# Dilated mixer: scores and outputs by residues modulo 4 in quarters of the array, with resident bias tables

## The chip, the cores and the metric

The kernel runs on one core of one Trainium2 chip. The metric is the device time of one execution in microseconds; the kernel before has a median of 881.81 us over three runs (881.51 to 882.02).

## What is computed

A batch of one sequence with 256 tokens of 1024 features passes two hybrid layers (retention, sparse attention and a gated recurrence side by side) and then a second block of two layers, all in float32. The first mixer of the second block is the dilated one, and it is where this change is:

```python
DSW_GROUPS = ((128, 1), (512, 4), (2048, 16))       # window, dilation
qkv = (h @ w_qkv).reshape(B, S, 3, G, Hg, HEAD_DIM) # 3 groups of 8 heads of 64
q, k = rmsnorm(q, q_gain), rmsnorm(k, k_gain)
# per group g: query t attends to t - dilation*i, i = 0..window/dilation
logits = q.k * SCALE + bias[t5_bucket(distance), 8*g + head]   # masked outside of the band
o_g, lse_g = softmax_attend(logits, v)
wts = softmax(stack(lse_g))                          # over the three groups
o = sum_g wts_g * o_g;  h = h + o @ w_o
```

A softmax over groups of softmaxes is one softmax over the logits of all three groups, and that is how both kernels compute it, head by head. With 256 tokens group 0 sees the last 129 tokens, group 1 every fourth token back to the start, and group 2 every sixteenth. So a query of groups 1 and 2 only meets keys that have its own residue modulo 4.

## The kernel before

Every engine has its own program, written out by hand; semaphores tie them. TensorE does the dense products as three fp32r products each (high by high, high by low, low by high part; lines 810 to 812 and 841 to 843). Weights come in chunks of 128x2048 through SyncE's queue; ScalarE writes the high part of a chunk (`split_hi`, L1465), VectorE the low part (`split_lo`, L1967), into a ring of four.

The dilated mixer starts with six blocks of 512 columns for q and k ("dsw" blocks 0 to 5; VectorE normalizes each, `qk_norm`), and the three v blocks 6 to 8. While the v blocks run, TensorE folds q and k to features by tokens (`fold`, 12 times 4 transposes, L758), copied out by ScalarE (L1683) and VectorE (L2334). Heads go in pairs p = 0 to 3 (e is the head of the pair, and its 64 features are one half of the rows of the array).

- `dil_pair_scores(p)`: per head, each of the three groups takes 256 keys for the second 128 queries (L1086) and 128 keys for the first 128 (L1093). Products of the masked pairs are computed too.
- `logits(u)` on VectorE: per head one operation on 768 and one on 384 columns (L2344) adds the bias and takes the row maximum. The bias tables have room for four heads; GpSimd brings each head's table from DRAM (`bias_vec`) once the head four before is done (L749).
- `softmax(u)` on ScalarE: exponentials of 768 and 384 columns (L1690, L1691). `scaled(u)` on VectorE divides by the sums (L2354 to L2356).
- `dil_transposes(u, g)`: three 128x128 transposes per head and group, copied out by ScalarE (L1696) or VectorE (L2360).
- `dil_output(p, g)`: the weighted sums of v (L1124, L1126), the two heads in two halves of the array's columns. `dil_high` and `dil_low` (L1675, L2326) then make the high and low parts for the product with `w_o` (block "dswo", `tokens(o, ...)`).

The order of all this on each engine is written in three functions called `dilated`, and each engine waits in that order. TensorE may begin `dil_transposes(0, 0)` only when ScalarE has emptied bank 0 of the last v block, `take(f + 8, 0)` (L1488), and `dil_transposes(1, 0)` after `take(f + 8, 1)`.

Early, in the first input block, VectorE adds bias rows and masks (`bias_vectors`, L2141, L2142), GpSimd writes them to `bias_vec` (L687, L688), and both ScalarE and VectorE wait for those transfers (`vec_out`) ahead of the sparse attention of layer 0 (before L1771 and L2470).

```python
for g in range(3):
    for e in range(2):
        o = dil_scores(e)[0][:, S * g:S * g + S]
        mm = pe.matmul(o.rearrange("p (t n) -> p t n", t=2), q(e, g, 1), k(e, g, slice(0, 2)), start=True, stop=True)
```

## Time and profile before

| what | value |
|---|---|
| median of three runs | 881.81 us |
| the profiled execution | 881.71 us |
| its span | 879.9 us |
| TensorE busy | 872.1 us (99%), 5546 products |
| VectorE, ScalarE busy | 620.2 us (70%), 491.7 us (56%) |
| GpSimd busy | 40.4 us (5%) |
| chain that ended last | TensorE 86%, VectorE 4%, ScalarE 4%, DMA 2% |

The execution's own time holds 1.8 us around its span. A product of float32 operands (not fp32r) stands in the trace as two instructions, so six calls of `pe.matmul` in a loop are a row with x12. Starts of consecutive rows of TensorE give what a piece costs there; the durations overlap.

### The profile page before, as it was taken

The numbers are of one execution on the slowest core, as the hardware profiler recorded it, in microseconds if no ns is written. First come the engines' busy times: TensorE is split into PE (matmuls) and PEld (weight loads), VectorE is DVE, ScalarE is ACT, GpSimd is POOL, SyncE is SP. The second block draws the span as 40 slices with busy tenths as digits, with TensorE's granted clock in tenths as the row PEclk, the third lists the DMA queues.
The fourth block names the chain that finished last, engine by engine and source line by source line (L and its number), as shares of the span: only waits on it lengthen the run. The fifth ranks groups of instructions, "written<-read, shape, count | busy, mean of one in ns | idle before, by whom it ended". The sixth has DMA issues, their size and how long they took to land.

```text
span 879.9 us, 13709 instructions
## 1 busy us (share of the span) xinstructions
PE 872.1 (99%) x5546; PEld 750.2 (85%) x5546; DVE 620.2 (70%) x1064; ACT 491.7 (56%) x742; POOL 40.4 (5%) x69
## 2 busy tenths in 40 slices
PE   9999999999999999999999999999999999999998
PEld 7887888987888888878999988888777899998886
DVE  5889987989988987776666644466778586664441
ACT  6566836667847654576555533355667565553330
POOL 1700010000000000100000000010000000000000
PEclk9999999999999999999999999999999999999999
DMA  8963255742344678623555565565553286555540
GB/s 299 332 230 112 99 192 149 240 144 97 104 160 168 239 233 228 185 74 126 191 183 187 186 202 196 196 191 189 168 168 120 96 279 195 189 182 194 170 156 24
DMA packets 79454, 155.54 MB, mean 177 GB/s; under 512 B 5644, under 2 KB 7852, under 8 KB 79392
## 3 DMA queue, kind: packets, MB, share of 16 engines
q1 hardware_dynamic: 75200, 142.81, 48.9%
q0 software_dynamic: 4192, 11.86, 5.1%
q8 instruction: 44, 0.72, 0.3%
q14 instruction: 18, 0.15, 0.0%
HBM read 153.55 MB, written 1.11 MB: 176 GB/s over the span
## 4 chain that ended last, share of the span: by engine, by line
PE 86%; DVE 4%; ACT 4%; issue 2%; DMA 2%; POOL 1%; SPq 0%; DVEq 0%; ACTq 0%
PE ps L810 17%; PE ps L812 16%; PE ps L811 16%; PE ps L841 9%; PE ps L842 8%; PE ps L843 8%; PE ps_mid L758 2%; DVE w_lo L1967 2%; ACT w_hi L1465 2%; DMA w_raw<-in_w_in 1%; PE ps_mid L1004 1%; PE ps L758 1%; PE ps_mid L1034 1%; PE ps_mid L810 1%; ACT y_tok L1600 1%
## 5 line engine op out<-in xcount | busy, mean ns | idle before, releaser
L1967 DVE TENSOR_TENSOR w_lo<-w_raw,w_hi 128x2048 fp32r<-128x2048 f32 x133 | 299.7, 2260 | 144.0 <-ACT w_hi L1465 143.8
L1465 ACT ACTIVATE w_hi<-w_raw 128x2048 fp32r<-128x2048 f32 x133 | 250.8, 1891 | 189.9 <-PE ps L812 141.5
L810 PE MATMUL ps<-w_hi,act_hi 128*128 128x512 f32 (+1 forms) x446 | 177.6, 398 | 0.8 <-DVE w_lo L1967 0.4
L812 PE MATMUL ps<-w_hi,act_lo 128*128 128x512 f32 (+1 forms) x446 | 171.2, 384 | 0.0
L811 PE MATMUL ps<-w_lo,act_hi 128*128 128x512 f32 (+1 forms) x446 | 170.8, 383 | 0.0
L810 PE MATMUL ps<-w_hi,hid 128*128 128x512 f32 x296 | 116.1, 392 | 0.0
L812 PE MATMUL ps<-w_hi,hid 128*128 128x512 f32 x296 | 115.2, 389 | 0.0
L811 PE MATMUL ps<-w_lo,hid 128*128 128x512 f32 x296 | 115.2, 389 | 0.0
L841 PE MATMUL ps<-act_hi,w_hi 128*128 128x256 f32 x384 | 109.9, 286 | 1.0 <-ACT gate_c L1492 1.0
L843 PE MATMUL ps<-act_hi,w_lo 128*128 128x256 f32 x384 | 107.6, 280 | 0.0
L842 PE MATMUL ps<-act_lo,w_hi 128*128 128x256 f32 x384 | 107.6, 280 | 0.0
L810 PEld LDWEIGHTS ps<-w_hi,act_hi 128*128 128x128 f32 x446 | 83.7, 188 | 19.7 <-issue 2.8
L812 PEld LDWEIGHTS ps<-w_hi,act_lo 128*128 128x128 f32 x446 | 83.7, 188 | 16.8
L811 PEld LDWEIGHTS ps<-w_lo,act_hi 128*128 128x128 f32 x446 | 83.9, 188 | 13.8
L841 PEld LDWEIGHTS ps<-act_hi,w_hi 128*128 128x128 f32 x384 | 72.4, 189 | 2.4 <-issue 1.6
L842 PEld LDWEIGHTS ps<-act_lo,w_hi 128*128 128x128 f32 x384 | 72.5, 189 | 0.1
L843 PEld LDWEIGHTS ps<-act_hi,w_lo 128*128 128x128 f32 x384 | 72.5, 189 | 0.0
L841 PE MATMUL ps<-early_acts,w_hi 128*128 128x256 f32 x256 | 71.7, 280 | 0.0
L843 PE MATMUL ps<-early_acts,w_lo 128*128 128x256 f32 x256 | 71.5, 279 | 0.0
L842 PE MATMUL ps<-early_acts,w_hi 128*128 128x256 f32 x256 | 71.5, 279 | 0.0
L810 PEld LDWEIGHTS ps<-w_hi,hid 128*128 128x128 f32 x296 | 55.6, 188 | 12.0 <-issue 0.8
L812 PEld LDWEIGHTS ps<-w_hi,hid 128*128 128x128 f32 x296 | 55.6, 188 | 11.6
(354 smaller groups left out, 1200.3 us busy)
## 6 DMA issues: line engine op xcount, KB each, us to landing
w_raw<-in_ffn_w SPq DMA_DIRECT2D x64, 1024.0 KB, 5.3
w_raw<-in_w_in SPq DMA_DIRECT2D x21, 1024.0 KB, 6.1
w_raw<-in_a_w_qkv SPq DMA_DIRECT2D x18, 1024.0 KB, 5.1
w_raw<-in_b_w_qkv SPq DMA_DIRECT2D x12, 1024.0 KB, 5.0
w_raw<-in_w_out SPq DMA_DIRECT2D x8, 1024.0 KB, 5.1
w_raw<-in_b_w_o SPq DMA_DIRECT2D x4, 1024.0 KB, 5.0
w_raw<-in_w_in SPq DMA_DIRECT2D x12, 256.0 KB, 6.0
w_raw<-in_w_in SPq DMA_DIRECT2D x4, 512.0 KB, 3.6
```

The source lines that it names most:

```text
L758: return pe.transpose(bank[:, at:at + 128].bitcast(FR), src, ident_r[:, :])
L810: pe.matmul(o, ah, wh, start=first, stop=False)
L811: pe.matmul(o, ah, wl, start=False, stop=False)
L812: mm = pe.matmul(o, al, wh, start=False, stop=last)
L841: pe.matmul(o, wh, ah, start=k == 0 and f % 2 == 0, stop=False)
L842: pe.matmul(o, wh, al, start=False, stop=False)
L843: mm = pe.matmul(o, wl, ah, start=False, stop=k == 7 and f % 2 == 1)
L1004: pe.matmul(nsa_scores(2 * p + e)[0], q[e][:, 128:256], k[e][:, :], start=True, stop=True)
L1034: pe.matmul(o[64 * e:64 * e + 64, :], v(0, e), nsa_turned(2 * p + e)[:, 0:S], start=p % 4 == 0, stop=False)
L1465: act.activation(w_hi[:, c % RING, :, 0:n], w_raw[:, c % RAW, :, 0:n], ACT.Copy).then_inc(w_hi_done, 1)
L1600: ins = act.activation(y[:, i % 2, 128 * k:128 * k + 128], act_bank[i][:, 128 * k:128 * k + 128], ACT.Identity, bias=gs[:, 1, kt:kt + 1], ...
L1967: dve.tensor_tensor(lo, w_raw[:, c % RAW, :, 0:n], hi.bitcast(F), ALU.subtract).then_inc(w_lo_done, 1)
```

## The change

- Scores: a head's queries are taken by residue modulo 4. For each half t (residues t and 2+t), group 0 multiplies 64 queries with all 256 keys, and groups 1 and 2 with the 64 keys of their own residue only. Each product has 64 features and 64 queries, so it fills a quarter of the array (row half: head e, column half: r). Scores are 2 x 384 columns per head rather than 768 + 384.
- The weights, exponentials and divisions shrink to 2 x 384 columns; the weights of a pair are turned in three parts of four transposes (n = 3p, 3p+1: group 0 of each head; n = 3p+2: groups 1 and 2 of both), copied out as 128x512.
- Output: `dil_near_output(p)` for group 0 (column halves), `dil_far_output(p)` for groups 1 and 2 in quarters. Sums are kept by residues in two banks, and `dil_high` and `dil_low` write them back in order of tokens.
- The v blocks of groups 1 and 2 (blocks 7, 8) are computed with tokens in the order of residues: ScalarE and VectorE write reordered copies of the activations (`mixed_high`, `mixed_low`), and TensorE reorders the row scale with 8 products against columns of the identity (`rstd_in_residues`).
- All heads' bias tables are resident in three rooms, filled by 18 DMAs; the bias rows are added in the dsw stage, and the waits for `vec_out` in layer 0 are gone.
- The order on each engine is rewritten.

```diff
@@ laid_out
+    near, own, far = [a["rel_bias_2"][buckets(d)].T for d in distances()]
@@ gpsimd
-                if l == 0:
-                    pool.wait_ge(vec_sb, 1)
-                    pool.dma_start(bias_vec[0:24], vec[0:24, 0, :]).then_inc(vec_out, 16)
-                    pool.dma_start(bias_vec[24:40], vec[0:16, 1, :]).then_inc(vec_out, 16)
...
+                pool.wait_ge(ttr_done, UNIT0[2])
+                pool.dma_start(vec[0:16], dram["bias_rows"]).then_inc(rows_in, 16)
+                pool.dma_start(allowed[0:16], dram["c_allowed"]).then_inc(allowed_in, 16)
+                pool.wait_ge(vec_sb, 1)
+                pool.dma_start(bias_vec[:, :], vec[0:16]).then_inc(vec_out, 16)
+                pool.wait_ge(vec_out, 16)
+                for i, (u0, n, room) in enumerate(DIL_ROOMS):
+                    if i == 0:
+                        pool.wait_ge(x_new, TT * LAYERS)
+                    elif i == 1:
+                        pool.wait_ge(ssq_done, 1)
+                    else:
+                        pool.wait_ge(qk_norm, 6)
+                    for r in range(2):
+                        rows = room[64 * r:64 * r + 64].rearrange("p (u n) -> p u n", u=n)
+                        near = bass.AP(bias_vec.tensor, u0 * 1152 + 2 * r, [[4, 64], [1152, n], [1, 257]])
+                        pool.dma_start(rows[:, :, 128:385], near).then_inc(dil_bias_in[i], 16)
+                        far = bass.AP(bias_vec.tensor, u0 * 1152 + 896, [[2, 64], [1152, n], [1, 128]])
+                        for at in (0, 385):
+                            pool.dma_start(rows[:, :, at:at + 128], far).then_inc(dil_bias_in[i], 16)
@@ tensor
+            def rstd_in_residues():
+                pe.wait_ge(rstd_done, 1)
+                for a in range(2):
+                    for t in range(2):
+                        for h in range(2):
+                            mm = pe.matmul(ps7[64 * a + 32 * t:64 * a + 32 * t + 32, h:h + 1], ident[:, 2 * h + a:2 * h + a + 125:4], rstd[:, 0, t:t + 1],
+                                           start=True, stop=True)
+                mm.then_inc(rstd_mixed_ps, 1)
@@ dil_pair_scores
+                q = lambda e, g, i: qkv[row(e), p % 2, 512 * g + 256 * (p // 2) + i:512 * g + 256 * (p // 2) + 253 + i:4]
+                for t in range(2):
+                    for r in range(2):
+                        for e in range(2):
+                            pe.matmul(near_scores(e, t)[row(r)], q(e, 0, 2 * r + t), keys(e), start=True, stop=True)
+                for t in range(2):
+                    for g in (1, 2):
+                        for r in range(2):
+                            for e in range(2):
+                                i = 2 * r + t
+                                mm = pe.matmul(far_scores(e, t, g)[row(r)], q(e, g, i), k(e, g, i), start=True, stop=True)
+                mm.then_inc(s_ready, 2)
@@ outputs
+            def dil_near_output(p):
+                if p:
+                    pe.wait_ge(pair_lo, p)
+                turned_out(3 * p)
+                turned_out(3 * p + 1)
+                for chunk in range(2):
+                    for t in range(2):
+                        for e in range(2):
+                            c0 = 512 * 6 + 64 * (2 * p + e)
+                            pe.matmul(ps_mid[64 * e:64 * e + 64, 2048 + 512 * t + 128 * p:2176 + 512 * t + 128 * p],
+                                      qkv[:, chunk, c0:c0 + 64], dil_turned(3 * p + e)[:, 256 * chunk + 128 * t:256 * chunk + 128 * t + 128],
+                                      start=chunk == 0, stop=False)
+            def dil_far_output(p):
+                turned_out(3 * p + 2)
+                pt = dil_turned(3 * p + 2)
+                for g in (1, 2):
+                    for r in range(2):
+                        for t in range(2):
+                            for e in range(2):
...
+                                mm = pe.matmul(ps_mid[64 * e:64 * e + 64, at:at + 64], qkv[64 * t:64 * t + 64, r, c0:c0 + 64],
+                                               pt[64 * t:64 * t + 64, 256 * e + 128 * (g - 1) + 64 * r:256 * e + 128 * (g - 1) + 64 * r + 64],
+                                               start=False, stop=g == 2 and r == 1)
@@ dilated, TensorE
-                ahead(21)
+                ahead(20)
+                rstd_in_residues()
+                ahead(1)
...
+                dil_transposes(0)
                 dil_pair_scores(2)
                 pe.wait_ge(acc_free[1], free_count(o))
+                dil_transposes(1)
+                dil_transposes(2)
+                dil_near_output(0)
+                dil_transposes(3)
+                dil_pair_scores(3)
+                dil_far_output(0)
+                dil_transposes(4)
+                dil_transposes(5)
+                dil_transposes(6)
+                dil_near_output(1)
+                dil_far_output(1)
+                dil_transposes(7)
+                dil_transposes(8)
+                tokens(o, 0, (0,))
                 tokens(o, 1, (0,))
...
@@ dilated, ScalarE
+            def mixed_high():
+                act.wait_ge(vec_out, 16)
+                act.activation(tables_turn[:, 0:2048].rearrange("p (k r i) -> p k r i", r=4, i=64),
+                               act_hi.rearrange("p k (i r) -> p k r i", r=4), ACT.Copy).then_inc(mixed_hi_done, 1)
...
                 softmax(1)
                 splits(f + 8, 0)
+                softmax(2)
+                softmax(3)
                 take(f + 8, 0)
-                softmax(2)
                 take(f + 8, 1)
-                transposed(0, 0)
...
@@ dilated, VectorE
                 logits(2)
                 logits(3)
                 scaled(2)
+                scaled(3)
                 logits(4)
-                scaled(3)
-                transposed(0, 2)
                 logits(5)
-                transposed(3, 0)
+                transposed(1)
+                logits(6)
                 scaled(4)
+                transposed(4)
                 dil_low(0)
...
@@ hybrid, ScalarE and VectorE
-                act.wait_ge(vec_out, 32)
-                dve.wait_ge(vec_out, 32)
```

Two places of the order follow. The first is ScalarE around the last v block: the rows of bank 0 and 1 of that block are `area<-ps,rstd` (before) and `area<-ps,rstd_mixed` (now), and the exponentials are `area,den<-area,ttr_min`. Before:

```order
L1465 ACTIVATE w_hi<-w_raw 128x2048 [waits w_used,w_arrived2]
L1488 ACTIVATE area<-ps,rstd 128x512 [waits rstd_done,acc_ready]
L1690 ACTIVATE area,den<-area,ttr_min 128x768 [waits ttr_done]
L1691 ACTIVATE area,den<-area,ttr_min 128x384
L1488 ACTIVATE area<-ps,rstd 128x512 [waits rstd_done,acc_ready]
L1696 ACTIVATE area<-ps 128x384 [waits t_ready]
```

The same place now:

```order
L1526 ACTIVATE w_hi<-w_raw 128x2048 [waits w_used,w_arrived2]
L1763 ACTIVATE area,den<-area,ttr_min 128x384 [waits ttr_done]
L1763 ACTIVATE area,den<-area,ttr_min 128x384
L1763 ACTIVATE area,den<-area,ttr_min 128x384 [waits ttr_done]
L1763 ACTIVATE area,den<-area,ttr_min 128x384
L1552 ACTIVATE area<-ps,rstd_mixed 128x512 [waits rstd_mixed_done,rstd_done,acc_ready] x2
L1768 ACTIVATE area<-ps 128x512 [waits t_ready]
```

Both banks of the v block are now emptied behind the exponentials of heads 2 and 3, where bank 0 stood ahead of them. TensorE at the start of the part without dense products, where it waits for those banks (`acc_free0`, `acc_free1`); the order lists a float32 product once. Before:

```order
L812 MATMUL ps<-w_hi,act_lo 128x512
L758 MATMUL ps<-ident_r,hid 128x128 [waits p_scaled,acc_free0]
L758 MATMUL ps<-ident_r,hid 128x128 x2
L1086 MATMUL ps_mid<-area 128x256 [waits ttr_done]
L1086 MATMUL ps_mid<-area 128x256 x5
L1093 MATMUL ps_mid<-area 128x128 x4
L1093 MATMUL ps_mid<-area 128x128 [waits shared_bank]
L1093 MATMUL ps_mid<-area 128x128
L758 MATMUL ps<-ident_r,hid 128x128 [waits p_scaled,acc_free1]
```

Now:

```order
L852 MATMUL ps<-w_hi,early_acts 128x512
L793 MATMUL ps<-ident_r,hid 128x128 [waits p_scaled,acc_free0]
L793 MATMUL ps<-ident_r,hid 128x128 x3
L1140 MATMUL ps_mid<-area 64x256 [waits ttr_done]
L1140 MATMUL ps_mid<-area 64x256 x7
L1146 MATMUL ps_mid<-area 64x64 x16
L793 MATMUL ps<-ident_r,hid 128x128 [waits p_scaled,acc_free1]
L793 MATMUL ps<-ident_r,hid 128x128 x3
L793 MATMUL ps<-ident_r,hid 128x128 [waits pt_a]
L793 MATMUL ps<-ident_r,hid 128x128 x3
L1181 MATMUL ps_mid<-area 64x128 [waits pt_d,pt_a]
L1181 MATMUL ps_mid<-area 64x128 x7
```

The transposes come in fours instead of threes, the scores are 24 products instead of 12, and the first output stands behind copies of both engines.

## Rows read from the trace of the kernel before

**Rows 1.** The page: busy time of TensorE, and its granted clock in 40 slices

```profile
PE 872.1 (99%) x5546; PEld 750.2 (85%) x5546; DVE 620.2 (70%) x1064; ACT 491.7 (56%) x742; POOL 40.4 (5%) x69
...
PEclk9999999999999999999999999999999999999999
```

**Rows 2.** Stretches: length; PE, PEld, DVE, ACT, POOL busy; PEclk, DMA, GB/s

```profile
345.00:373.85 28.85, 28.85 (x183) 23.61 (x182) 21.93 (x34) 15.95 (x24) 3.00 (x4) 1.00 0.69 189
373.85:399.45 25.60, 24.91 (x229) 18.44 (x228) 17.89 (x48) 17.62 (x45) 0.79 (x2) 1.00 0.21 64
```

**Rows 3.** Waits of TensorE: us in total, times, longest

```profile
PE ps L758 <- ACT area L1696: 0.7, 2, 0.4
```

**Rows 4.** Timeline of TensorE, a pair's scores: start, us, what

```profile
359.64 1.57 PE L1086 MATMUL ps_mid<-area 64*128 64x256 f32 x12
361.04 0.83 PE L1093 MATMUL ps_mid<-area 64*128 64x128 f32 x12
361.80 0.50 PE L810 MATMUL ps<-w_hi,act_hi 128*128 128x512 f32 x1
```

**Rows 5.** Timeline of TensorE, the part without dense products

```profile
379.25 0.65 PE L1124 MATMUL ps<-area 128*64 128x256 f32 x4
...
380.05 0.81 PE L758 MATMUL ps<-ident_r,hid 128*128 128x128 f32 x6
...
392.14 0.70 PE L758 MATMUL ps<-ident_r,hid 128*128 128x128 f32 x6
392.68 0.67 PE L758 MATMUL ps_mid<-ident_r,hid 128*128 128x128 f32 x6
...
395.50 0.65 PE L1124 MATMUL ps<-area 128*64 128x256 f32 x4
...
396.20 0.60 PE L1124 MATMUL ps<-area 128*64 128x256 f32 x4
```

**Rows 6.** Timeline of TensorE: products of 32 columns of weights, four at a time

```profile
51.30 1.10 PE L1328 MATMUL ps<-area 128*32 128x64 f32 x64
52.33 0.39 PE L841 MATMUL ps<-act_hi,w_hi 128*128 128x256 f32 x1
```

**Rows 7.** Timeline of ScalarE: exponentials, a weight split, a 128x512 copy

```profile
307.57 0.60 ACT L1501 ACTIVATE area<-ps 128x512 f32<-128x512 f32 x1 [0.74 <-PE ps L812]
...
364.19 0.94 ACT L1690 ACTIVATE area<-area,ttr_min 128x768 f32<-128x768 f32 x1 [3.71 <-DVE ttr_min L2344]
...
366.65 0.60 ACT L1691 ACTIVATE area<-area,ttr_min 128x384 f32<-128x384 f32 x1
...
367.25 1.89 ACT L1465 ACTIVATE w_hi<-w_raw 128x2048 fp32r<-128x2048 f32 x1
```

**Rows 8.** Timeline of VectorE in the mixer

```profile
351.93 0.69 DVE L2334 COPY area<-ps 128x512 f32<-128x512 f32 x1 [1.43 <-PE ps L758]
...
363.60 0.55 DVE L2344 CUSTOM_DVE_ANT_1 area<-ps_mid,area 128x384 f32<-128x384 f32 x1
364.08 0.08 DVE L2344 DVE_READ_ACCUMULATOR2_ANT ttr_min<- 128x1 f32 x1
...
369.18 2.29 DVE L1967 TENSOR_TENSOR w_lo<-w_raw,w_hi 128x2048 fp32r<-128x2048 f32 x1 [0.65 <-ACT w_hi L1465]
...
382.13 0.41 DVE L2356 TENSOR_SCALAR tables<-tables,rden 128x384 f32<-128x384 f32 x1
```

**Rows 9.** Timelines of ScalarE, VectorE, TensorE in the first input block

```profile
32.41 0.60 ACT L1771 ACTIVATE area<-ps_mid 128x512 f32<-128x512 f32 x1 [1.09 <-DMA bias_vec<-area]
...
34.84 4.50 DVE L1967 TENSOR_TENSOR w_lo<-w_raw,w_hi 128x2048 fp32r<-128x2048 f32 x2 [0.53 <-ACT w_hi L1465]
...
42.66 0.48 PE L1004 MATMUL ps_mid<-area 64*128 64x256 f32 x1 [0.67 <-DVE area L2470]
```

**Rows 10.** Timelines of VectorE and GpSimd in the dsw stage: slack, and a table's DMA

```profile
328.61 2.29 DVE L1967 TENSOR_TENSOR w_lo<-w_raw,w_hi 128x2048 fp32r<-128x2048 f32 x1 [1.69 <-ACT w_hi L1465]
...
373.12 0.76 POOL L749 DMA_DIRECT2D y_tok<-bias_vec  x1 [6.55 <-DVE ttr_min L2344]
```

More of the change, by code:

```diff
@@ L89, in laid_out @@
     a = {n: np.asarray(inputs[n]) for n in PARAMS}
-    a["bias_rows"] = a.pop("rel_bias_2")[buckets(np.arange(384) - 127)].T
+    near, own, far = [a["rel_bias_2"][buckets(d)].T for d in distances()]
+    a.pop("rel_bias_2")
+    pairs = np.stack([far[16:24], far[8:16]], 2).reshape(8, 256)
+    a["bias_rows"] = np.concatenate([near[0:16], own[0:16], np.concatenate([pairs, pairs])], 1)
     pos = a.pop("nsa_cmp_pos").reshape(LAYERS, 2, 16, 2, HD)
@@ L223, in empties @@
         if ph == 2:
[L224 to L226 removed]
+            return "ada"[u % 3]
         return "a"
     ORDER = [(ph, u, 0) for ph in (0, 1) for u in range(16)]
[L230 removed]
+    ORDER += [(2, n, 0) for n in range(12)]
     ORDER += [(3, u, 0) for u in range(16)]
@@ L415, in build @@
         bias_in = [sem(f"bias_in{i}") for i in range(4)]
-        shared_bank = sem("shared_bank")
+        dil_bias_in = [sem(f"dil_bias_in{i}") for i in range(3)]
+        rstd_mixed_ps = sem("rstd_mixed_ps")
+        rstd_mixed_done = sem("rstd_mixed_done")
+        mixed_hi_done = sem("mixed_hi_done")
+        mixed_lo_done = sem("mixed_lo_done")
         fold_ps = sem("fold_ps")
@@ L792, in token_steps @@
                         pe.wait_ge(w_lo_done, split_count(c))
+                    if b == FIRST["dsw"] + 7 and half == 0 and k == 0:
+                        pe.wait_ge(mixed_hi_done, 1)
+                        pe.wait_ge(mixed_lo_done, 1)
                     if b in (FIRST["dswo"], FIRST["mobao"]):
@@ L805, in token_steps @@
                         ah, al = mixed_operand(k, half)
+                    elif b in (FIRST["dsw"] + 7, FIRST["dsw"] + 8):
+                        ah, al = [v[:, 128 * half:128 * half + 128] for v in mixed_acts(k)]
                     else:
@@ L1089, in dil_pair_scores @@
-                for g in range(3):
-                    for e in range(2):
-                        if g == 2 and e == 0:
-                            pe.wait_ge(shared_bank, p + 1)
-                        mm = pe.matmul(dil_scores(e)[1][:, 128 * g:128 * g + 128], q(e, g, 0), k(e, g, 0), start=True, stop=True)
-                mm.then_inc(s_ready, 2)
-            def part_emptied(u, g):
-                engine, n = emptied_by(2, u, g)
-                pe.wait_ge({"a": pt_a, "d": pt_d}[engine], n)
@@ L1100, in dil_transposes @@
-            def dil_transposes(u, g):
-                if u >= 6 and g == 1:
-                    pe.wait_ge(ttr_done, UNIT0[2] + 8)
-                elif g:
-                    part_emptied(u, 0 if u >= 6 else g - 1)
-                else:
-                    pe.wait_ge(p_scaled, UNIT0[2] + u + 1)
-                    if u >= 2:
-                        part_emptied(u - 2, 2)
-                for i, at in enumerate((768 + 128 * g, S * g, S * g + 128)):
-                    mm = turn(t_bank(2, u, g), 128 * i, dil_weights_turn(u, at))
+                row = lambda e: slice(64 * e, 64 * e + 64)
@@ new lines, in dil_transposes @@
+            def dil_transposes(n):
+                p, part = n // 3, n % 3
+                bank = t_bank(2, n, 0)
+                if part < 2:
+                    pe.wait_ge(p_scaled, UNIT0[2] + 2 * p + part + 1)
+                if n >= 2:
+                    turned_out(n - 2)
+                if part < 2:
+                    for chunk in range(2):
+                        for t in range(2):
+                            mm = turn(bank, 256 * chunk + 128 * t, dil_weights_turn(2 * p + part, 0, t, chunk))
+                else:
+                    for e in range(2):
+                        for g in (1, 2):
+                            mm = turn(bank, 256 * e + 128 * (g - 1), dil_weights_turn(2 * p + e, g, None))
@@ L1930, in _ @@
                     normalized_scaled(l, t)
-            gemms("dsw", 6, begin=lambda: square_sums(0))
+            gemms("dsw", 6, begin=lambda: square_sums(0), also={(4, 0): mixed_high})
             dilated()
```

287 lines of the change are left out of this document (126 added, 161 removed).

## The prediction

> **What bounds the kernel now.** I read the page first, then busy time by stretch, TensorE's waits, and the timelines of the three engines between 345 and 400 us. TensorE is busy 99% of the span and its granted clock is 1.00 of full speed, the upper of its two levels, in every slice [rows 1]. So the time is TensorE's work, and a change counts by what it takes off that work, less the idle time that it brings. The dilated mixer has two stretches [rows 2]. Up to 373.85 us folds and the first two pairs' scores lie between dense products; what leaves TensorE there is gained at once, unless somebody else's result is then late. From 373.85 to 399.45 us, 25.6 us, TensorE turns weights, takes the last scores and forms outputs, with only four dense steps between. There ScalarE and VectorE are busy 17.6 and 17.9 us, each handing pieces to TensorE. TensorE's waits for ScalarE's copies are 0.7 us in all [rows 3], so the three engines are nearly balanced in that part. That is the point to watch: a shorter TensorE part can turn into waits.
>
> **Work taken off TensorE.** A pair's scores cost 2.16 us from start to the next product [rows 4], for 3 x (256+128) = 1152 columns per head, two heads at once. One output piece costs 0.80 us for 384 columns [rows 5]. A price per column and a fixed price through both: 1.77 ns per column and 0.12 us for entering and leaving. I take it that four quarters run at once as two halves do. Then:
> - Scores: group 0 is two sets of four quarters of 256 columns, groups 1 and 2 four sets of 64: 768 columns, 1.48 us. Saved 0.68 x 4 = 2.7 us.
> - Outputs: before 12 x 0.80 = 9.6. Now per pair a near piece of 512 columns (1.03 us) and a far piece of four sets of 64 (0.57): 6.4. Saved 3.2 us.
> - Transposes: 72 become 48. Six take 0.54 us from row to row [rows 5], 0.09 each. Saved 2.2 us.
> - `rstd_in_residues`: 8 products with one column in another shape of the array. No row has this; 16 instructions at the 16 ns of the closest packed group [rows 6] are 0.26, and entering and leaving 0.24. I take 0.5 us; 0.3 and 1.2 (at 63 ns per instruction, 12 in 0.76 us [rows 4]) are the ends.
>
> Work off TensorE: 2.7 + 3.2 + 2.2 - 0.5 = 7.6 us.
>
> **What the new order gives back.** I walk the chain with the durations of the rows. Exponentials of 384 columns take 0.60 us, so a head's are 1.20 (before 3.06 for two heads, 364.19 to 367.25) [rows 7]; one logit operation of 384 columns is 0.48, a head's 0.96; dividing a head about 1.0, a 128x512 copy on VectorE about 0.6 after overlap [rows 8], on ScalarE 0.5.
> - ScalarE's weight split behind softmax 0 and 1 started at 367.25 [rows 7]. The reordered row scale puts it 0.6 later, shorter logits 0.4 and shorter exponentials 0.65 earlier: 366.8. It takes 1.8, VectorE's half of the split 2.2 [rows 8]: 371.0. Logits of head 2: 371.9. Now softmax 2 and 3, 2.4: 374.4. Only then is bank 0 of the last v block emptied, 0.6: 375.1. TensorE, ready at about 372.9, waits for it 2.3 us. Before, that bank was emptied ahead of both exponentials.
> - Transposes 0, scores of pair 2: results at 377.2. VectorE takes logits 4 and 5 (1.9) before it copies part 1 (0.6): first output at 379.9. TensorE, with parts 1 and 2 turned by 377.9, waits 2.0.
> - Near output 0 (1.0), part 3 (0.5), scores of pair 3 (1.5): 382.9, far output and two parts more: 384.2. Part 6 needs the bank that VectorE empties behind logits 6, scaled 4 (383.1 + 1.0 + 1.0 + 0.6 = 385.7). Waits 1.6.
> - From there no copy is late: part 6, near and far 1, parts 7 and 8, two dense steps, near 2, part 9, far 2, parts 10 and 11, two steps, near and far 3 are 9.9 us: 395.7, against 399.45 before [rows 2].
>
> So three waits of 5.9 us replace some 2 us of small ones, and of 7.6 us about half arrives: **-3.7 us**. If ScalarE's and VectorE's pieces were each 15% slower, the chain would give back 0.8 more.
>
> **The first input block.** ScalarE waits 1.09 us there for the transfer of the bias vector, VectorE then 0.53 us for ScalarE's weight split, and TensorE 0.67 us for VectorE [rows 9]. Without `vec_out` VectorE's splits start 0.53 earlier. Between nothing (if its next input from TensorE is what comes last) and 0.67 I take **-0.5 us**.
>
> **What is costed at nothing.** VectorE gets the add of 1152 columns and copies of 2048 columns in the dsw blocks; by the split of 2048 columns in 2.29 [rows 8] at most 1.3 + 2.3 us. It waits 1.69 us for ScalarE in a block's period there [rows 10], so three blocks absorb them, and the ring holds four chunks. `mixed_high` on ScalarE costs about one split, 1.9 us [rows 7]; that engine is 56% busy [rows 1]. Uncovered, the 3.6 us would all be TensorE's. GpSimd issues 18 bias DMAs and 3 more at about 0.76 us [rows 10]; the last six start when q and k are normalized, before 351.9 [rows 8], 4.6 us of issues, while head 6 is wanted at 383. The output's high and low parts read and write in steps now (nearest rows are unit steps of the same size); twice their time moves the end by 0.3 us.
>
> **The sum** goes against the profiled execution: 881.7 - 3.7 - 0.5 = **877.5 us**. That execution lies 0.1 us below the median, so the same number stands for a median.
>
> **The rivals.**
> 1. *A floor per small product.* A far piece has 32 instructions of 64 columns, 14 ns apart at 1.77 ns per column. The nearest row is 64 instructions of 64 columns in 1.03 us, 16 ns each, four at once, but with 32 columns of weights [rows 6]; no row has quarters, or operands in steps of four. If loading twice as many weights or the steps set the pace, at 28 ns, twice the columns' price, a far piece would last 0.90 instead of 0.45. Of the eight, the two ahead of 373.85 hide in TensorE's first wait, and the walk then gives -1.3 - 0.5: **879.9 us**. The Trainium skill (TensorE: Matmul & The Clock Gate, "Wait — 56ns, not 53.3ns?") states such a floor: starts of matmuls are never closer than about 25 ns; and TensorEngine Tiling (Array Packing), "Instruction Overhead", advises not to take a tiling factor from a dimension that is already small. By that page the time would be an estimated 879.4, about this rival's; the trace's 16 ns [rows 6] speaks against it.
> 2. *The waits don't come.* If ScalarE and VectorE finish early enough, all 7.6 + 0.5 arrive: 873.6. For it: both are only 70% busy in that stretch [rows 2] and their work shrinks. Against it: the three waits come from the written order, not from load. Some of it may shrink: **874.5 us**.
> 3. *Quarters run two at a time*, not four: scores take 2.7, far outputs 0.85, and the walk ends 0.65 later than before: **881.9 us**, no change. For it: rows show two row halves [rows 4] and four column strips [rows 6], none shows both splits together.
> 4. *Slower.* If start to start of an instruction in quarters is what the scores of 128 columns show, 63 ns (12 in 0.76 us [rows 4]), then scores are 3.0, near outputs 1.0, far outputs 2.0 us: the walk gives +6.9 - 0.5, **888.1 us**. That row is explained by its columns (two at once), so little speaks for it; it decides from about 40 ns on, where nothing is left of the gain.
>
> **How the numbers follow.** Forecast 0.58, rival 1 0.14, rival 2 0.12, rival 3 0.09, rival 4 0.07. A difference under 0.2% (1.8 us) can't be told from no change. Faster: forecast, rivals 1 and 2, and nothing of the rest, less a little for slow tails of the first: 0.83. Same: 0.10. Slower: 0.07. The range reaches from rival 2's 874.5 to a little short of rival 3: slower copies (+0.8), a dearer row scale (+0.7) and half of the floor (+1.2) with no gain in the first block (+0.5) give 880.7; I round up to 881.0.
>
> **What would show it.** In the profile after: four transposes in 0.36 us; a pair's scores, 48 instructions, in 1.4 to 1.6 us; near outputs about 1.0, far outputs 0.45 to 0.6 (0.8 to 1.0 is rival 1, over 1.5 rival 4). A wait of about 2.3 us before the first transposes of weights, on ScalarE's copy of the v block (absent in rival 2), about 2.0 before the first near output and 1.6 before part 6, both on VectorE's copies. The stretch from the last v product to the output's last piece about 3.7 us nearer to the start, plus 0.5 from the first block, where ScalarE's wait for `bias_vec` is gone. Wrong would be: TensorE waiting for a bias room, a clock below 1.00 in the part with waits, or VectorE late for q and k.

## The result and the profile after

The changed kernel takes **885.11 us** (median of six runs, 883.95 to 887.35) against 881.94 of the kernel before in six runs beside it: a ratio of 1.0037, with a 95% interval of 1.0027 to 1.0047. It is slower by 0.4%; the forecast was a faster kernel, 877.5 us with a range up to 881.0. The profiled execution is the slowest of the six: 887.35 us, its span 885.6 us.

The page of the changed kernel, where rows 1 stood before:

```profile
PE 871.6 (98%) x5730; PEld 751.8 (85%) x5730; DVE 618.4 (70%) x1061; ACT 491.4 (55%) x736; POOL 44.5 (5%) x78
```

TensorE is busy about as long as before (871.6 us to 872.1), with 184 more instructions, and the span is 5.7 us longer: that is idle time. Part of the busy time is spent at the lower clock, as the stretches below show, so the work did shrink. TensorE's waits in the changed kernel (total, times, longest), against the single line of [rows 3] in the mixer:

```profile
PE ps_mid L793 <- DVE area L2328: 2.9, 1, 2.9
PE ps_mid L1181 <- DVE area L2434: 1.8, 1, 1.8
PE ps L793 <- DVE tables L2434: 1.2, 1, 1.2
...
PE ps L793 <- ACT area L1552: 0.7, 1, 0.7
PE ps L850 <- ACT area L1568: 0.7, 1, 0.7
```

Lines 2 to 4 are the three waits of the forecast, at the places it named: before the first output, part 6, and the first transposes. Line 1 is no part of the mixer: it is at 51.61 us, in the first input block. To find where the time goes I hold the same five events of several kernels side by side, in us from the start of the span. The dsw mark is a product early in that stage that waits 0.21 to 0.25 us for VectorE's weight split in every kernel. The last two rows are experiments, below.

| kernel | dsw mark | first fold | first transposes of weights | first output | first product behind the last output | span |
|---|---|---|---|---|---|---|
| before | 274.58 | 346.13 | 373.85 | 377.81 | 398.65 | 879.9 |
| changed | 278.96 | 352.10 | 380.58 | 385.95 | 404.45 | 885.6 |
| changed, second trace | 277.28 | 349.42 | 377.90 | 383.28 | 401.90 | 883.9 |
| q1_aligned | 274.35 | 346.48 | 374.95 | 380.33 | 397.48 | 878.6 |
| h6_all | 274.03 | 346.52 | 372.99 | 376.58 | 393.19 | 874.7 |

So 4.4 us (2.7 in the second trace) are lost ahead of the dsw mark, where the diff seems to do little but take a wait away. From the first fold to behind the last output the changed kernel takes 52.35 us, and the kernel before took 52.52. Almost nothing of the forecast's gain arrived, and there are two separate questions.

**The first block.** Two stretches, before and then changed (length; PE, PEld, DVE, ACT, POOL busy; granted clock, DMA share, GB/s):

```profile
32.00:43.00 11.00, 9.59 (x82) 9.08 (x82) 10.30 (x13) 7.06 (x10) 7.97 (x14) 1.00 1.04 360
43.00:60.00 17.00, 17.00 (x188) 14.84 (x185) 13.89 (x44) 11.77 (x33) 0.00 (x0) 1.00 0.76 284
```

```profile
32.00:43.00 11.00, 9.93 (x85) 9.43 (x85) 10.71 (x13) 5.79 (x9) 8.09 (x14) 1.00 1.05 267
43.00:60.00 17.00, 14.06 (x159) 12.90 (x157) 11.89 (x34) 9.18 (x22) 0.00 (x0) 0.90 0.78 288
```

The DMA engines are full in both between 32 and 43 us, but move 267 GB/s instead of 360. Between 34 and 36 us GpSimd's queue is all but alone on them (SyncE's moves 0.02 MB there in the changed kernel). It brings the compression weights, `in_nsa_cmp_w` into the tile `cw`: two transfers of 512 KB, in pieces of 256 bytes. The queue's packets, MB and share, before and changed:

```profile
q0 software_dynamic: 179, 0.67, 100.9%
```

```profile
q0 software_dynamic: 124, 0.47, 105.4%
```

In the same 2 us 30% less arrives. The median time from issue to landing of the two transfers is 6.2 us before and 7.8 in the changed kernel, and behind them come the dense products' weights. ScalarE's split of such a chunk in the kernel before:

```profile
41.62 1.91 ACT L1465 ACTIVATE w_hi<-w_raw 128x2048 fp32r<-128x2048 f32 x1 [3.53 <-DMA w_raw<-in_w_in]
```

In the changed kernel ScalarE, VectorE and TensorE then wait one for the other:

```profile
46.52 1.91 ACT L1526 ACTIVATE w_hi<-w_raw 128x2048 fp32r<-128x2048 f32 x1 [8.19 <-DMA w_raw<-in_w_in]
...
48.47 2.29 DVE L2032 TENSOR_TENSOR w_lo<-w_raw,w_hi 128x2048 fp32r<-128x2048 f32 x1 [4.77 <-ACT w_hi L1526]
...
51.61 0.62 PE L793 MATMUL ps_mid<-ident_r,early_acts 128*128 128x128 f32 x3 [2.94 <-DVE area L2328]
```

Behind that wait the granted clock falls as well: it is 0.50 from 52 to 54 us (0.90 over the whole stretch from 43 to 60). In the second trace the wait is 1.6 us, the clock stays at 1.00, and the loss is 2.7 us instead of 4.4.

**The mixer.** TensorE's timeline in the changed kernel, where rows 4 and 5 stood:

```profile
350.93 0.44 PE L1122 MATMUL ps_mid<-rstd,ident 128*32 128x1 f32 x16
351.30 0.50 PE L850 MATMUL ps<-w_hi,tables_turn 128*128 128x512 f32 x1
...
365.63 1.16 PE L1140 MATMUL ps_mid<-area 64*64 64x256 f32 x16
366.61 1.13 PE L1146 MATMUL ps_mid<-area 64*64 64x64 f32 x32
367.67 0.50 PE L850 MATMUL ps<-w_hi,tables_turn 128*128 128x512 f32 x1
...
380.58 0.53 PE L793 MATMUL ps<-ident_r,hid 128*128 128x128 f32 x4 [0.74 <-ACT area L1552]
381.04 1.16 PE L1140 MATMUL ps_mid<-area 64*64 64x256 f32 x16
...
385.95 1.97 PE L1181 MATMUL ps_mid<-area 128*64 128x128 f32 x16 [1.77 <-DVE area L2434]
387.85 0.75 PE L793 MATMUL ps<-ident_r,hid 128*128 128x128 f32 x4
...
393.62 0.50 PE L793 MATMUL ps<-ident_r,hid 128*128 128x128 f32 x4 [1.25 <-DVE tables L2434]
...
398.20 1.09 PE L1181 MATMUL ps_mid<-area 128*64 128x128 f32 x16
399.23 0.53 PE L793 MATMUL ps<-ident_r,hid 128*128 128x128 f32 x4
399.69 0.69 PE L1195 MATMUL ps_mid<-area 64*64 64x64 f32 x32
400.32 1.09 PE L793 MATMUL ps<-ident_r,hid 128*128 128x128 f32 x8
```

A pair's scores take 2.04 us, not 1.48: the near part 0.98 as forecast, the 32 far products 1.06 instead of 0.45. Far outputs, also 32 products of 64 columns, take 0.63. The near output at 398.20 takes the forecast 1.03, but the one at 385.95, right behind a wait of 1.77 us, takes 1.90. The granted clock is 0.50 from 386 to 389 us, the lower of its two levels, and 0.72 over this stretch:

```profile
384.00:390.00 6.00, 4.23 (x50) 3.38 (x53) 1.80 (x7) 3.58 (x10) 0.00 (x0) 0.72 0.01 3
```

### The profile page after: what moved, and what is told of

The parts are those of the page before. It is cut to its first block, busy times and chain, and to the rows that moved or that the text cites. A ratio compares the mean times of both kernels' runs of the same rounds, so it can differ in the third digit from the quotient of the medians.

```text
span 885.6 us, 14060 instructions
## 1 busy us (share of the span) xinstructions
PE 871.6 (98%) x5730; PEld 751.8 (85%) x5730; DVE 618.4 (70%) x1061; ACT 491.4 (55%) x736; POOL 44.5 (5%) x78
## 4 chain that ended last, share of the span: by engine, by line
PE 82%; DVE 8%; ACT 4%; DMA 3%; issue 2%; ACTq 0%; DVEq 0%
PE ps L850 15%; PE ps L852 14%; PE ps L851 14%; PE ps L881 9%; PE ps L883 8%; PE ps L882 8%; DVE w_lo L2032 3%; PE ps_mid L793 3%; DMA w_raw<-in_w_in 2%; ACT w_hi L1526 2%; DMA w_raw<-in_a_w_qkv 1%; PE ps_mid L1044 1%; PE ps_mid L1074 1%; ACT y_tok L1666 1%; PE ps_mid L1496 1%
## 5 line engine op out<-in xcount | busy, mean ns | idle before, releaser
L850 PE MATMUL ps<-w_hi,act_hi 128*128 128x512 f32 (+1 forms) x414 | 164.1, 396 | 1.1 <-ACT area L1568 0.7
L852 PE MATMUL ps<-w_hi,act_lo 128*128 128x512 f32 (+1 forms) x414 | 158.7, 383 | 0.0
L851 PE MATMUL ps<-w_lo,act_hi 128*128 128x512 f32 (+1 forms) x414 | 158.3, 382 | 0.0
L852 PE MATMUL ps<-w_hi,hid 128*128 128x512 f32 x316 | 123.1, 390 | 0.0
L850 PE MATMUL ps<-w_hi,hid 128*128 128x512 f32 x296 | 116.1, 392 | 0.0
L850 PEld LDWEIGHTS ps<-w_hi,act_hi 128*128 128x128 f32 x414 | 77.7, 188 | 19.0 <-issue 2.8
L852 PEld LDWEIGHTS ps<-w_hi,act_lo 128*128 128x128 f32 x414 | 77.7, 188 | 15.6
L851 PEld LDWEIGHTS ps<-w_lo,act_hi 128*128 128x128 f32 x414 | 77.9, 188 | 13.2
L852 PEld LDWEIGHTS ps<-w_hi,hid 128*128 128x128 f32 x316 | 59.3, 188 | 12.6
L850 PEld LDWEIGHTS ps<-w_hi,hid 128*128 128x128 f32 x296 | 55.5, 188 | 11.8 <-issue 0.8
```

Of the source, the lines that this page charges most:

```text
L850: pe.matmul(o, ah, wh, start=first, stop=False)
L851: pe.matmul(o, ah, wl, start=False, stop=False)
L852: mm = pe.matmul(o, al, wh, start=False, stop=last)
```

## The experiments

### The first block: what slows the transfers

The first three runs are the changed kernel once more, the changed kernel with the old first block put back in it, and the reverse: the kernel before without its two waits at that place.

> The changed kernel as it is, once more, for its second trace. Theory A (the first input block now lets the weight transfers collide with GpSimd's, whatever the execution): 884 to 886 us, and again 3 to 5 us more than before by 60 us of the span, with ScalarE waiting 5 us or more for a weight chunk near 45 us. Rival B (the stall of 4.4 us was one execution's accident): the loss by 60 us is under 1 us in this trace, and the time is spread out between executions.

Measured: 885.63 us (883.78 to 887.09), ratio 1.0040 (1.0028 to 1.0051); 270 GB/s between 32 and 43 us, ScalarE's wait 6.9 us, 2.70 us lost at the dsw mark. The loss is not an accident of one execution.

```
+ pool.dma_start(old_rows[0:24], ...); pool.dma_start(old_allowed[0:24], ...)     # same sizes, same place as before
...
# in words: DVE adds them, pool writes 36 and 24 KB to DRAM, ACT, DVE and PE wait as before
```

> The changed kernel with the old first input block put back as a dummy: the same two early loads, the addition, the two writes to DRAM and the waits of the three engines for them. Theory A: the stall of the first block goes, 880.5 to 881.5 us, and the products behind the first block stand where they stood in the kernel before. Rival B: no change against the changed kernel, within 1 us.

Measured: 884.95 us, ratio 1.0042 (1.0028 to 1.0055), 273 GB/s, 2.92 us lost at the mark. Theory A fell.

```
- vec = cut(TT * PW + 6144, 768, ...)         - act.wait_ge(vec_out, 32); dve.wait_ge(vec_out, 32)   (ahead of the transposed copies)
+ vec = cut(18240, 768, ...)                  + the same two waits ahead of the first unit
```

> The kernel before with only the two waits for the bias vector moved from ahead of the transposed copies to ahead of the first unit (the vector in another room). Theory A in its strong form (the waits were what kept the transfers apart): slower by 2 to 4.5 us, 884 to 886. Rival (what counts is the early loads and the later start of GpSimd's row of small transfers): 881.4 to 882, or the 0.5 us faster that the prediction gave.

Measured: 881.36 us, ratio 0.9993 (0.9984 to 1.0003), 363 GB/s. The dsw mark comes 0.58 us earlier than before, close to the 0.5 us of the forecast; that is one trace, and the medians can't tell it from nothing. The loss belongs to something that all forms of the changed program share. Five guesses at it follow.

```
+ a["bias_rows"] padded to 48 rows; bias_vec of 48 rows                 (in the kernel before)
```

> The kernel before, with only its tensor of bias rows in DRAM and the internal bias vector made as large as the changed kernel's (zeros behind, never read; the loads are those of before). Theory P (the larger tensors shift what lies behind them in DRAM, and the transfers of 32 to 44 us then run slower): 32 to 43 us at about 270 GB/s instead of 360, a third weight transfer of about 15 us instead of 9.8, and 883 to 886 us. Rival Q (something in the changed program itself): 360 GB/s and 881.4 to 882.2 us.

Measured: 881.79 us, ratio 1.0000 (0.9991 to 1.0010), 364 GB/s.

```
- a["bias_rows"] of 16 x 1152        + a["bias_rows"] of 16 x 576, and a["bias_rest"] of 16 x 576 behind all inputs
```

> The changed kernel, its bias rows cut in two tensors: the first as large as before's, at the same place of the list, the rest behind all others (one more load, behind layer 1). The internal bias vector keeps its new size. Theory P, if the input's size is what counts: 360 GB/s between 32 and 43 us, no wait of 1.5 to 3 us near 50 us, 880.5 to 882.5 us. Rival Q, or if the internal tensor counts: no change against the changed kernel, 884 to 887.

Measured: 885.32 us, ratio 1.0033 (1.0023 to 1.0043), 262 GB/s.

```
- six transfers per room (64 rows x n x 257 or 128)       + one transfer per room (128 rows x n x 512)
```

> The changed kernel, each room of bias tables filled by one transfer of 128 rows in place of six (it leaves out the right tables). Theory S (the new forms of GpSimd's transfers change what its queue does everywhere): 350 GB/s or more between 32 and 43 us, and no wait near 50 us. Rival: still 260 to 275 GB/s there.

Measured: 268 GB/s, 885.6 us in one run.

```
- for g in (1, 2): for r in range(2): ...     + one g, one r        (far scores and far outputs)
```

> The changed kernel with 192 far products left out (three of four far scores and outputs), so that TensorE's program is no longer than before's. Theory T (the longer program moves what lies in DRAM): 350 GB/s or more between 32 and 43 us. Rival: still 260 to 275 GB/s. In the mixer itself the two uncovered score pieces and the far outputs shrink by about 0.6 us each.

Measured: 268 GB/s, 883.6 us in one run.

```
+ a = {"pad": np.zeros((16, 5000)), ...}       ahead of all inputs, and one load from it behind layer 1
```

> The changed kernel with a tensor of 320 KB put ahead of all inputs (one load of 72 KB from it behind layer 1, overwritten before use). Theory U (the places of the inputs in DRAM decide how fast the transfers of 32 to 43 us run): some other rate than 260 to 275 GB/s there. Rival: the same rate.

Measured: 269 GB/s, 887.1 us in one run. All five fell. What was left was where the tiles of the two programs lie. The kernel has a padding, `to_line`, in front of its big tiles. The diff takes 2 columns from it for the 2 columns of `rstd_mixed`, as if the sum stayed. But the 8 bytes of `rstd_mixed` push the next tile 32 bytes on; every tile in these programs begins on a multiple of 32 bytes. Their addresses in the two built programs:

```
                 rstd_mixed   to_line   x_res             area
before                -        17856    18432 = 36 x 512  143872
changed             17856      17888    18464             143904
```

Every tile behind the padding lies 32 bytes further. `cw` begins 57600 bytes into `area`, so its 256-byte pieces began on multiples of 256 and no longer do. The next runs change only the padding.

```
- sb("to_line", [128, 142])        + sb("to_line", [128, 136])       (changed kernel, q1)
- sb("to_line", [128, 144])        + sb("to_line", [128, 152])       (kernel before, q2)
```

> The changed kernel with the padding ahead of the big tiles cut from 142 to 136 columns, which puts them back on the addresses of the kernel before (the first at 18432 bytes, a multiple of 512, in place of 18464). Theory V (the shift by 32 bytes slows the transfers of small pieces): 355 to 365 GB/s between 32 and 43 us, no wait near 50 us, the first dsw product at 273.5 to 274.6 us instead of 277.3 to 279, and 880 to 882 us. Rival: unchanged, 257 to 273 GB/s and 884 to 887 us.

> The kernel before with the padding grown from 144 to 152 columns, which moves its big tiles by the same 32 bytes and changes nothing else. Theory V: 257 to 273 GB/s between 32 and 43 us, and 2.5 to 4.5 us slower than before, 884 to 886.5 us. Rival: 360 GB/s and 881.4 to 882.2 us.

Measured: q1 882.05 us (880.44 to 882.54), ratio 0.9998 (0.9989 to 1.0007); q2 885.76 us, ratio 1.0040 (1.0024 to 1.0055). The same stretch in q1, then in q2:

```profile
32.00:43.00 11.00, 9.99 (x85) 9.48 (x85) 10.71 (x13) 6.50 (x10) 8.11 (x14) 1.00 1.05 355
```

```profile
32.00:43.00 11.00, 9.35 (x79) 8.87 (x78) 9.53 (x9) 5.67 (x9) 8.09 (x14) 1.00 1.05 280
```

The padding alone turns 267 GB/s into 355 in the one and 360 into 280 in the other, and carries 3.1 us out of the changed kernel (885.11 to 882.05; 3.6 against e1's median) and 4.0 into the kernel before (881.79 to 885.76). The two transfers of `cw` land in 6.0 us in q1 and 8.0 in q2. The dense products' weights, in pieces of 2 KB, don't mind: the 64 chunks of `in_ffn_w` land in 5.3 us in the kernel before and in the changed one, and in 5.4 in q2. Which places are good was asked in the kernel before, with 128 and 80 columns:

> The kernel before with its big tiles 64 bytes lower (padding of 128 columns in place of 144), so that none of them begins on a multiple of 256 bytes. If pieces of 256 bytes cost more whenever they begin off a multiple of 256: 255 to 275 GB/s between 32 and 43 us and 884 to 886.5 us, as with the shift by 32. If a multiple of 64 is enough: 360 GB/s and 881.4 to 882.2 us.

> The kernel before with its big tiles 256 bytes lower (padding of 80 columns), on multiples of 256 but not of 512 bytes. If multiples of 256 are what counts: 360 GB/s between 32 and 43 us and 881.4 to 882.2 us. If multiples of 512 count: some rate below 340 GB/s and up to 886 us.

Measured: 64 bytes lower 884.41 us, ratio 1.0029 (1.0017 to 1.0040); 256 bytes lower 882.13 us, ratio 1.0004 (0.9995 to 1.0013). The stretch in q3, then in q4:

```profile
32.00:43.00 11.00, 9.07 (x76) 8.58 (x74) 9.77 (x11) 5.67 (x9) 7.79 (x14) 1.00 1.06 282
```

```profile
32.00:43.00 11.00, 9.41 (x81) 8.93 (x80) 10.15 (x11) 7.40 (x10) 8.02 (x14) 1.00 1.05 366
```

Being off by 64 bytes is as bad as by 32, and by 256 costs nothing; 128 was not tried. The Trainium skill (DMA: Bandwidth & Descriptors, "How a descriptor splits into AXI transactions") states such a boundary for reads: a transaction must begin on a multiple of 256 bytes, so a piece of 256 bytes that begins elsewhere lies in two. Here it is the written side, in SBUF, that moved, and the same boundary shows in the rates; that the same splitting is the cause was not shown.

### The mixer: what the far products cost

```
- k(e, g, i)        + qkv[row(e), p % 2, c0:c0 + 64]
```

> The changed kernel, far scores with 64 adjacent keys as the moving operand in place of every fourth (it leaves out that the keys are those of the residue; queries stay in steps of four). Theory C (the step of 16 bytes in the moving operand sets the 33 ns): the 32 far products of a pair take 0.45 to 0.55 us instead of 1.06, and the kernel gains up to 1.2 us (the two pairs behind the dense part; the other two hide in the wait before the first transposes). Rival (sixteen-way start cost or the stepped stationary operand): still about 1.0 us per pair and no gain.

Measured: 32 products in 1.00 us (1.06 before the edit), 885.86 us. The keys' step is not the cause, or not alone. So the next kernel has four forms, one for each pair:

```
if p in (0, 2): queries in unit steps    if p in (1, 2): result in unit steps    if p == 2: keys too
```

> The changed kernel with its four pairs' far scores in four forms (it leaves out the right queries, keys or places of the scores): pair 0 with queries in unit steps, pair 1 with the result written in unit steps, pair 2 with queries, keys and result in unit steps, pair 3 as it is (32 products in about 1.05 us). If the stepped load of the queries sets the 33 ns, pairs 0 and 2 take 0.45 to 0.65 us; if the result in steps of two does, pairs 1 and 2; if it is neither (a price of the start of each product in quarters by rows), all four take about 1.0 us.

Measured, pairs 0, 1 and 2 with the product behind each:

```profile
365.47 1.11 PE L1155 MATMUL ps_mid<-area 64*64 64x64 f32 x32
366.51 0.50 PE L850 MATMUL ps<-w_hi,tables_turn 128*128 128x512 f32 x1
...
372.55 1.13 PE L1155 MATMUL ps_mid<-area 64*64 64x64 f32 x32
373.61 0.50 PE L850 MATMUL ps<-w_hi,tables_turn 128*128 128x512 f32 x1
...
380.83 0.65 PE L1155 MATMUL ps_mid<-area 64*64 64x64 f32 x32
381.41 0.81 PE L793 MATMUL ps<-ident_r,hid 128*128 128x128 f32 x6
```

From start to start of the next row that is 1.04 us, 1.06 and, with nothing in steps, 0.58. Next comes each step by itself:

> The changed kernel, far scores with a single operand in steps each (it leaves out the right queries, keys or places): pair 0 only the queries in steps of four, pair 1 only the keys, pair 2 only the result in steps of two, pair 3 none. One stepped operand among three was not enough to undo: with queries, with keys or with the result made unit-stepped alone the 32 products still took 1.00 to 1.06 us, all unit-stepped 0.58. Theory: each step by itself brings the price of about 31 ns per product, so pairs 0, 1 and 2 take about 1.0 us and pair 3 about 0.58. Rival: two of the three steps are needed, and one or more of pairs 0 to 2 takes about 0.6.

```profile
364.25 1.07 PE L1155 MATMUL ps_mid<-area 64*64 64x64 f32 x32
365.25 0.50 PE L850 MATMUL ps<-w_hi,tables_turn 128*128 128x512 f32 x1
...
371.29 1.11 PE L1155 MATMUL ps_mid<-area 64*64 64x64 f32 x32
372.33 0.50 PE L850 MATMUL ps<-w_hi,tables_turn 128*128 128x512 f32 x1
...
379.62 0.65 PE L1155 MATMUL ps_mid<-area 64*64 64x64 f32 x32
380.20 1.09 PE L793 MATMUL ps<-ident_r,hid 128*128 128x128 f32 x8
```

With only the queries in steps of four the piece takes 1.00 us, with only the keys in steps of four 1.04, and with only the result in steps of two 0.58. So two thirds of the theory held: either operand read in steps of 16 bytes nearly doubles the piece, and undoing only one gives almost nothing, but the written step is free. (Pair 3, 0.86 us, lies where the clock had fallen, and is left out.)

### The mixer: the order, and all of it together

```
PE:   - T0, S2, T1, T2, near 0, T3, S3, far 0, T4      + T0, T1, S2, T2, near 0, far 0, T3, T4, S3
ACT:  - softmax 2, 3, take(f+8,0), take(f+8,1), transposed 0     + take(f+8,0), softmax 2, take(f+8,1), transposed 0, softmax 3, ...
DVE:  - logits 4, 5, transposed 1, logits 6, scaled 4, transposed 4   + transposed 1, ..., logits 4, 5, scaled 4, transposed 4, ..., logits 6
```

(T: transposes of a part, S: scores of a pair.)

> The changed kernel in another order behind the v blocks: bank 0 of the last v block is emptied ahead of the exponentials, part 1 is turned and copied ahead of the scores of pair 2, parts 3 and 4 are turned ahead of the scores of pair 3, and VectorE divides head 4 and copies part 4 ahead of logits 6 and 7. If the three waits (0.74, 1.77 and 1.22 us of TensorE) and the clock's fall behind the second are what the mixer lost: 3.7 us less, and up to 1.4 more where the clock fell; 880.5 to 882 us. If the engines are too busy, the waits move and under 1.5 us is gained.

Measured: 881.16 us, ratio 0.9991 (0.9981 to 1.0000), 4 us below the changed kernel. From the first fold to behind the last output it takes 47.95 us (52.35 in the changed kernel, 52.52 before). TensorE's waits of 3.7 us there are down to 0.7, the longest 0.5. Against the changed kernel's stretch where the clock stays up (51.00, in e2 and q1) that is 3.05 us: the waits. The rest is the clock, which doesn't fall in this trace.

> The changed kernel in the order of h1_order, and aligned as q1_aligned. If the two gains are independent: h1_order's 881.2 less 2 to 3 us of the first block, 878 to 879.2 us. If the shift is not the cause: 881.2 again.

Measured: 877.70 us, ratio 0.9949 (0.9936 to 0.9963). The two gains add up: it is 4.35 us below q1.

```
+ return [c0, c0 + 128], room.rearrange("p j (r i) -> p j i r", r=4) if q or at else room     (folded)
- q, k: [c + i : c + i + 253 : 4]           + q, k: [c + 64 * i : c + 64 * i + 64]            (far scores, and q of the near ones)
```

> As h5_order_aligned, and the folds write all queries and the keys of groups 1 and 2 residue by residue, so that the far scores read both in unit steps (the result stays the reference's). By the far products alone (32 in 0.58 us instead of 1.04): pairs 0 and 1 (hidden no longer, since the wait they hid in is gone) and pairs 2 and 3 give 0.46 each, 1.8 us less than h5: 876.3 to 877.5 us. If the copies of the folds, which now write in steps (mixed_high took 3.9 us in steps where a split takes 1.9), hold TensorE up: no better than h5 or worse.

Measured: **876.35 us** (875.64 to 876.79), ratio 0.9934 (0.9922 to 0.9947): the fastest version here. Scores of a pair are now 1.49 us:

```profile
360.05 1.09 PE L1141 MATMUL ps_mid<-area 64*64 64x256 f32 x16
360.96 0.64 PE L1147 MATMUL ps_mid<-area 64*64 64x64 f32 x32
361.54 0.50 PE L851 MATMUL ps<-w_hi,tables_turn 128*128 128x512 f32 x1
```

ScalarE's copies of the folds rise from 0.69 to about 1.2 us and VectorE's from 0.69 to 1.1; TensorE waits for none of them. Of the expected 1.8 us 1.35 arrive; a wait that grew took its share. The first wait of the two below is 0.2 us in h5, the second 0.5 in both:

```profile
PE ps L794 <- ACT area L1769: 1.1, 1, 1.1
PE ps L794 <- ACT area L1553: 0.5, 1, 0.5
```

## Why the prediction was wrong, step by step

Three steps failed. The sum had no term for the shift of the tiles by 32 bytes (3.1 us); the walk sized its pieces too small, the scores above all, and read its gain against the wrong end; and the waits were priced by their length alone, without the clock behind them. Without the shift the kernel takes 882.05 us, still above the range, so the first step alone doesn't explain the miss.

**A cost that it didn't have: the 32 bytes, 3.1 us (q1).** The kernel's diff takes the padding `to_line` from 144 to 142 columns, and the forecast has no word on it. It is the largest error, and no rival had it: I asked what each moved instruction costs, and not what each moved address does.

**Scores: 2.04 us, not 1.48.** The price per column was right for products with unit steps (near 0.98, far without steps 0.58) and for four quarters at once, so rival 3 fell. It was wrong for operands in steps. Rival 1 named both the steps and a price of 28 ns; the rows give 33 (1.06 us by 32), and in the scores only. Saved were 4 x 0.12 = 0.5 us instead of 2.7. The rule that spoke against this change stands in the Trainium skill (SBUF — State Buffer, "Door 1: The DMA port swizzle", its note on cachelines): reads that move to a new 16-byte line each time pay for it, and four float32 are such a step. g2 agrees. The 25 ns floor that the forecast weighed (the Trainium skill, TensorE: Matmul & The Clock Gate, "Wait — 56ns, not 53.3ns?") is not there in quarters: 0.58 us by 32 is 18 ns.

**Outputs and transposes.** Near outputs take 1.03 us as forecast, far ones 0.63 (0.57): 3.0 saved of 3.2. Four transposes take 0.46, so 0.116 each and not 0.09. Those of before cost more than rows 5 told as well (the three at 373.85 take 0.38, the six at 378.61 take 0.64, 0.107 each), so 72 x 0.107 - 48 x 0.116 = 2.1 of 2.2 us were saved. But the walk set the cheap price against the real end of before, and so came out too early (below).

**The row scale** was +0.5 and is +0.58 (from the dsw mark to the first fold, 71.55 us before, 72.13 in q1). **The first block's wait** was -0.5; at the dsw mark it is -0.58 in e3 and -0.23 in q1.

**The walk.** The three waits came in the three places, 0.74, 1.77 and 1.25 us against 2.3, 2.0 and 1.6. The first is short because TensorE comes later: the two stretched score pieces ahead of it delay it by 1.1 us. Its end is set by ScalarE, and the first transposes stand 28.47 us behind the first fold in q1 where 28.5 was forecast. The later ones were not on time. On the time scale of the kernel before (q1 plus 0.23) part 6 begins at 386.9, not 385.7: 1.2 us late, of which the two stretched scores on the way are 1.0. From part 6 to behind the last output q1 takes 10.8 us, not 9.9: 24 transposes at 0.116 instead of 0.09 are 0.6 of it, three far outputs 0.2. And the end was read against the wrong mark: 399.45 is one dense step behind the last output, whose end is at 398.65. The walk's gain should have read 2.95, not 3.7 us.

**The clock.** Below 1.00 in the part with waits was named as what would prove the forecast wrong, and got no price. In the changed kernel, its second trace and p3 the clock fell to 0.50 for about three us behind the 1.77 us wait, and the stretch from first fold to behind the last output took 52.35, 52.48 and 51.85 us; in f2 it fell again behind the third wait, and the stretch took 53.50. In e2 and q1, with the same waits and a clock of 1.00, it took 51.00 and 51.00. So one fall costs 0.9 to 1.5 us and two 2.5. Eight of q1's ten executions show a mean clock of 0.996 to 0.998, with a median of 882.05 us, while the profiled one, the fastest, took 880.44. Time and mean clock don't go together in each of them (one took 882.54 at 1.00). In h1 they do: six executions at 1.000 took 880.00 to 881.30 us, the four at 0.998 took 882.19 to 882.66. So the clock is the likeliest cause of such differences and not a proven one, and why it falls in one execution and not in the next stays open.

**Costed at nothing.** The reordered copies, which read in steps of four as well, cost up to twice their price: on ScalarE `mixed_high` takes 3.90 us (forecast 1.9), on VectorE `mixed_low` 2.44 and 1.53 (forecast 2.3 together).

```profile
317.92 3.90 ACT L1742 ACTIVATE tables_turn<-act_hi 128x2048 fp32r<-128x2048 f32 x1 [0.37 <-DMA bias_vec<-tables]
```

```profile
323.07 2.44 DVE L2393 CAST hid<-act_lo 128x1280 fp32r<-128x1280 f32 x1
...
325.43 1.53 DVE L2395 CAST early_acts<-act_lo 128x768 fp32r<-128x768 f32 x1
```

They were hidden in q1 and the second trace, where the stretch from dsw mark to first fold is 72.13 and 72.14 us. In the profiled execution of the changed kernel it is 73.14, with TensorE's wait of 0.7 us for ScalarE's copy (L1568); why there and not in the others was not tried. No bias table was late.

**The sum.** Against before, at full clock, q1's trace gives: first block -0.23, row scale +0.58, fold to last output -1.52, together -1.2 us where -4.2 was forecast. The missing 3.0 are the wrong mark (0.8), the stretched scores on the path (1.0), the transposes' and far outputs' prices (0.8), the first block (0.3) and 0.1 to 0.2 that has no name. The clock's fall adds 0.9 to 1.5 in an execution that has it, which makes 881.5 to 882.1 of the 881.8; q1's median is 882.05. The shift of 32 bytes adds 3.1: 885.1. The parts come from medians and from single traces, so the last half microsecond is not settled.

## What to carry to other kernels

A new small tile moves every tile behind it: look at the addresses before and after, and keep what small DMA pieces are written to on multiples of 256 bytes, with the padding worked out from rounded sizes. A step of 16 bytes in either operand of a small product made it 1.8 times as long here, and one in a copy 1.6 to 2 times; put the step where it is free (the product's result) or hide it (the copy that lays the operand out). And a wait on TensorE has two prices, its length and the clock behind it: order the engines so that what TensorE needs next is copied first, which here was worth more (4.0 us from the changed kernel to h1, 4.35 from q1 to h5, the clock's part in both) than the unit-stepped products (1.35).

## What the runs showed of the hardware that I had not expected

- GpSimd's transfers with 256-byte pieces move 0.67 MB in 2 us with the pieces on multiples of 256 bytes in SBUF, and 0.47 MB when they lie 32 bytes off. A shift of 64 bytes is as slow (282 GB/s for the stretch from 32 to 43 us), one of 256 is free (366). Transfers with 2 KB pieces land in the same time (5.3 and 5.4 us).
- Products of 64 columns in quarters of the array take 18 ns each with unit-stepped operands and 31 to 33 ns with queries, keys or both in steps of four; undoing only one of the two gives at most 0.06 us of 1.06.
- Results written to PSUM in steps of two cost nothing (0.58 us either way).
- Behind the same 1.77 us wait the granted clock fell in some executions (to 0.50 from 386 to 389 us in the changed kernel) and stayed at 1.00 in others (e2, q1). A wait of 2.94 us in the first block had a fall to 0.50 behind it in the changed kernel, and one of 3.2 us in g1 had none.
